# Shifted norms whose low parts come from the high parts, and a first slot pair that runs chunk by chunk

## The chip, the core and the metric

The kernel is one program on one NeuronCore of a Trainium2 chip. The metric is the device time of an execution in microseconds (us). The engines are named as in the profile: PE is TensorE (PEld its weight load), DVE is VectorE, ACT is ScalarE, POOL is GpSimd, SP is SyncE, which issues most of the transfers.

## What is computed

A chain of seven stages works on a matrix x of 256 tokens by 1024 features, in float32: a feed-forward block (`ffn1`), a mixer of attention over selected keys and a gated recurrence (`mix1`), a second feed-forward block (`ffn2`), and twice a three-part mixer (`mix2_l`) followed by a mixture over learned experts (`peer_l`). Every stage begins with a norm. In the first three it is modulated with a scale and a shift that come from a conditioning vector:

```python
def rmsnorm(x, g):
    y = xf * lax.rsqrt(jnp.mean(xf * xf, axis=-1, keepdims=True) + EPS)
    return (y * g.astype(jnp.float32)).astype(x.dtype)

def modulate(h, shift, scale):
    return h * (1 + scale[:, None, :]) + shift[:, None, :]

h = modulate(rmsnorm(x, mix_pre_g[l]), m[3], m[4])
proj = h @ w_in[l]
...
h = modulate(rmsnorm(x, ffn2_pre_g[l]), m[6], m[7])
y = swiglu(h, ffn2_w_gate[l], ffn2_w_up[l], ffn2_w_down[l])
...
u = rms_norm(x, attn_norm_w) @ w_in        # the later four stages: no shift
```

## The kernel before, in words

**Split products.** Each float32 product of matrices is made of three matmuls on rounded operands. A value v is kept as a high part, v rounded to the matmul's format, and a low part, v minus the high part. For weights W and activations H the kernel adds up hi(W)·hi(H), lo(W)·hi(H) and hi(W)·lo(H). The tiles of the weights are `whi` and `wlo`. Those of the normed activations are `HH` and `HL`, two views of one tile that the profile calls `HT`.

**Slots.** The weights of all stages come as one stream of 765 slots of 128x1024, two to a transfer of 1 MB into a `raw` buffer. For slot i, ACT copies `raw` to `whi` (`hi`, line 312), DVE (in some slots POOL) makes `wlo` (`lo`, line 331), and PE uses both. There are three buffers of each (`NSPLIT`), so that hi(i+3) waits until PE has used slot i. A slot's product with H has 8 chunks of 128 features, three matmuls each, in `chan`, lines 349 to 351. Each engine carries out its own instructions in the order in which the code issues them; what it needs of another engine it waits for on a semaphore.

**The start of a stage.** PE turns the normed rows into features by rows in PSUM (`norm_turn`, line 523), in 4 banks with 2 chunks each. Then `HH` and `HL` are made, one instruction for each chunk of 128x256:
- With a shift (`mix1` and `ffn2`; `ffn1` has its own opening): ACT makes all eight `HH` (line 547). DVE first makes lo of the second slot, then computes each chunk once more in full precision into `f` = x·gain + shift (line 574). The low part is f minus HH, a step of its own: for chunks 1, 3 and 7 on DVE (line 581), for chunks 0, 2, 4, 5 and 6 on POOL (line 589).
- Without a shift (the later four stages): ACT makes four `HH` (line 544), DVE the other four (line 560), and DVE makes each `HL` in one step as x·gain minus HH (line 570).

**The first two slots.** Of the six stages after `ffn1`, each gives its first two slots, i and i+1, to `chan_pair` (line 395): 48 matmuls for two outputs. They run in three passes over the eight chunks: hi(W)·HH, then lo(W)·HH, then hi(W)·HL. Slot i+2 is next on PE, with `chan`, and its first product waits for hi and lo of that slot. Behind the norm, DVE's next work is lo(i+2) in `ffn2` and in the later stages. In `mix1` there are two small instructions ahead of it, which split a weight `wi` that SP loads (lines 1551 and 1554; the transfer is issued at line 1285).

Of the kernel before, what the change touches and what calls it, by code (L numbers as in the profile page):

```python
# [4 lines left out]
F32 = mybir.dt.float32  # L5
# [5 lines left out]
ALU = mybir.AluOpType  # L11
# [143 lines left out]
class Program:  # L155
# [227 lines left out]
    def chan_pair(self, e, i, n, outs, banks):  # L383

        k, one = self.k, banks[0] == banks[1]
        for a, b in ((0, 0), (1, 0), (0, 1)):
            for c in range(8):
                s, h = slice(c * 128, c * 128 + 128), (self.HH, self.HL)[b]
                for j in range(2):
                    first, stop = (a, b, c) == (0, 0, 0), (a, b, c) == (0, 1, 7)  # L390
                    for w in k.late((("hi", "lo")[a], i + j), (("hh", "hl")[b], n, c),
                                    *(self.free[banks[j]] if first else [])):
                        e.wait_ge(*w)
                    part = (self.whi, self.wlo)[a][:, (i + j) % NSPLIT, :]
                    t = e.matmul(outs[j], part[:, s], h[:, c, :], start=first and not (j and one),  # L395
                                 stop=stop and (j == 1 or not one))
        t.then_inc(*k.inc("pe_used", ("used", i)))
        k.same(("used", i + 1), ("used", i))
# [151 lines left out]
    def norm_apply_dve(self, e, n, gain, shift, f, need, end):  # L550


        k = self.k
        if shift is None:
            self.lo(e, end + 1)
            for c in (2, 3, 6, 7):
                b = c // 2
                for w in k.late(self.turned(n, b), *need):
                    e.wait_ge(*w)
                e.tensor_scalar(self.HH[:, c, :], self.ps[:, b, 256 * (c % 2):256 * (c % 2) + 256], gain[:, c:c + 1], None,  # L560
                                ALU.mult).then_inc(*k.inc("dve_hh", ("hh", n, c)))
        else:
            self.lo(e, end + 1)
        for b in range(4):
            for c in (2 * b, 2 * b + 1):
                src, g = self.ps[:, b, 256 * (c % 2):256 * (c % 2) + 256], gain[:, c:c + 1]
                for w in k.late(self.turned(n, b), ("hh", n, 2 * b + 1), ("hh", n, c), *need):
                    e.wait_ge(*w)
                if shift is None:
                    e.scalar_tensor_tensor(self.HL[:, c, :], src, g, self.HH[:, c, :].bitcast(F32), ALU.mult,  # L570
                                           ALU.subtract).then_inc(*k.inc("dve_h", ("hl", n, c)))
                    k.same(("applied", n, b), ("hl", n, c))
                else:
                    e.tensor_scalar(f[:, c, :], src, g, shift[:, c:c + 1], ALU.mult,
                                    ALU.add).then_inc(*k.inc("dve_f", ("f", n, c)))
                    k.same(("applied", n, b), ("f", n, c))
            for c in (2 * b, 2 * b + 1):
                if shift is not None and c in (1, 3, 7):
                    for w in k.late(("f", n, c), ("hh", n, c)):
                        e.wait_ge(*w)  # L580
                    e.tensor_tensor(self.HL[:, c, :], f[:, c, :], self.HH[:, c, :].bitcast(F32),
                                    ALU.subtract).then_inc(*k.inc("dve_h", ("hl", n, c)))

    def norm_apply_pool(self, e, n, f):
        k = self.k
        for c in (0, 2, 4, 5, 6):
            for w in k.late(("f", n, c), ("hh", n, c)):
                e.wait_ge(*w)
            e.tensor_tensor(self.HL[:, c, :], f[:, c, :], self.HH[:, c, :].bitcast(F32),
                            ALU.subtract).then_inc(*k.inc("pool_h", ("hl", n, c)))  # L590

# [510 lines left out]
    def ffn_pool(self, e, t):  # L1104
        k, n, opens = self.k, NORM[t.tag], t.first > 0
        if opens:
            self.opening_pool(e, t)
        else:
            self.norm_apply_pool(e, n, t.f)
        if opens:  # L1110
            for b in range(2):
                self.bias_rows_pool(e, b)
            self.settle(e)
            e.tensor_scalar(self.norms[:, :, :], self.norms[:, :, :], D ** 0.5, None, ALU.mult).then_inc(*k.inc("pool_setup", "norms"))
            lc = self.lc
            e.tensor_scalar(lc[:, 0:4], self.vec("lam"), -1.0, None, ALU.mult).then_inc(*k.inc("pool_setup", "-lam"))
            for seg in range(5):
                self.softplus_pool(e, "lam", lc[:, 0:4], lc[:, 4:8], self.lc_sp, ["-lam"], seg)
            for w in k.late(("lam", "softplus")):
                e.wait_ge(*w)  # L1120
            e.tensor_scalar(lc[:, 0:4], lc[:, 4:8], -8.0, None, ALU.mult).then_inc(*k.inc("pool_setup", "lc a"))
            for w in k.late("lc a"):
                e.wait_ge(*w)
            e.tensor_scalar(lc[:, 4:8], lc[:, 0:4], 2.0, None, ALU.mult).then_inc(*k.inc("pool_setup", "lc"))
        for tt in range(2):
            self.sums_pool(e, ("res", n + 1, tt), self.st[:, tt, 1, :])
            self.sums_pool(e, (n + 1, tt), self.st[:, tt, 0, :])
        self.lo(e, t.down + F_CH + 1, True)
# [567 lines left out]
    def mixer1_pool(self, e):  # L1696
        k, t = self.k, self.m1
        n, tag = t.n, t.tag
        for w in k.late(("bias rows", 0), ("bias rows", 1)):
            e.wait_ge(*w)  # L1700
        self.norm_apply_pool(e, n, t.f)
        for w in k.late(("hh", n, 7), ("hl", n, 7)):
            e.wait_ge(*w)
        e.memset(t.SC[:, :, :], 0.0).then_inc(*k.inc("pool_index", (tag, "zero")))
# [1483 lines left out]
```

## Time and profile before

| | us |
|---|---|
| median of 3 runs (range) | 2466.11 (2465.45 to 2466.92) |
| the profiled execution's own time | 2468.6 |
| its span, first to last instruction | 2466.4 |
| PE matmuls busy | 2418.4 |
| DVE busy | 1801.5 |
| ACT busy | 1268.8 |
| POOL busy | 264.8 |

Matmuls are pipelined: a row's duration runs from its start to its modelled end, so that rows of PE overlap. A new matmul starts every 0.12 us or so where the moving operand has 256 columns. In rows of the timeline, "x16" is a run of 16 like instructions, and a bracket says how long the engine was idle ahead of the row and what ended that.

### The profile page before, as it was taken

To read this page: it belongs to the slowest core of one execution; us is meant where nothing else is said; L and a number is where in the kernel's file an instruction comes from. 1 tells how busy PE (TensorE), PEld (TensorE's weight loads), DVE (VectorE), ACT (ScalarE), POOL (GpSimd) and SP (SyncE) were. 2 spreads that over 40 slices of the span, in tenths; PEclk is the share of its full clock that TensorE was granted. 3 is DMA by queue.
4 is the path that set the end of the run, shared out by engine and by line. 5 is a ranking of instruction groups with operands and counts; after the bars stand their busy time and mean duration, and the time that the engine had idled before them with its cause. 6 is when DMAs were issued, how large, how long until landed. Compare 5 with 4: busy or idle time off the path is not lost.

```text
span 2466.4 us, 39282 instructions
## 1 busy us (share of the span) xinstructions
PE 2418.4 (98%) x15784; PEld 2102.4 (85%) x15784; DVE 1801.5 (73%) x3475; ACT 1268.8 (51%) x1811; POOL 264.8 (11%) x247
## 2 busy tenths in 40 slices
PE   7999999999999999999999999999999999999999
PEld 7987878988988888888888888988888888888887
DVE  8887666656756788888887556845778888888555
ACT  3544655445655565555444545654565555444444
POOL 3012101000203600000000000211720000000000
PEclk9999999999999999999999999999999999999999
DMA  9797334655324454444545555324454444445554
GB/s 388 264 341 256 122 123 174 222 197 176 127 107 173 175 192 181 171 171 156 186 171 201 196 190 197 138 103 170 173 188 172 174 170 171 171 174 185 205 190 151
DMA packets 73029, 455.77 MB, mean 185 GB/s; under 512 B 9099, under 2 KB 15371, under 8 KB 20754
## 3 DMA queue, kind: packets, MB, share of 16 engines
q1 hardware_dynamic: 72162, 452.21, 50.7%
q8 instruction: 127, 2.08, 0.3%
q0 software_dynamic: 688, 1.06, 0.3%
q14 instruction: 52, 0.43, 0.1%
HBM read 449.17 MB, written 4.06 MB: 184 GB/s over the span
## 4 chain that ended last, share of the span: by engine, by line
PE 89%; DVE 6%; ACT 3%; DMA 1%; issue 1%; POOL 1%; SPq 0%; DVEq 0%; ACTq 0%; POOLq 0%
PE ps L376 19%; PE ps L349 17%; PE ps L351 17%; PE ps L350 17%; PE ps L378 8%; PE ps L2559 2%; DVE wlo L331 2%; PE ps L375 1%; ACT whi L312 1%; DVE raw L342 1%; PE ps L395 1%; PE ps L1901 1%; DMA raw<-in_ffn_d 1%; PE ps L1151 1%; PE ps L2539 1%
## 5 line engine op out<-in xcount | busy, mean ns | idle before, releaser
L312 ACT ACTIVATE whi<-raw 128x1024 fp32r<-128x1024 f32 x765 | 809.5, 1060 | 1049.0 <-PE ps L351 639.5
L331 DVE TENSOR_TENSOR wlo<-raw,whi 128x1024 fp32r<-128x1024 f32 x700 | 856.6, 1227 | 516.0 <-ACT whi L312 515.6
L376 PE MATMUL ps<-HT,whi 128*128 128x512 f32 x2048 | 718.6, 399 | 0.0
L378 PE MATMUL ps<-HT,wlo 128*128 128x256 f32 x1792 | 502.1, 280 | 0.0
L376 PEld LDWEIGHTS ps<-HT,whi 128*128 128x128 f32 x2048 | 372.3, 188 | 68.9
L349 PE MATMUL ps<-whi,CT 128*128 128x512 f32 x1024 | 404.0, 395 | 1.2 <-DVE wlo L331 0.9
L350 PE MATMUL ps<-wlo,CT 128*128 128x512 f32 x1024 | 398.7, 389 | 0.0
L351 PE MATMUL ps<-whi,CT 128*128 128x512 f32 x1024 | 398.6, 389 | 0.0
L378 PEld LDWEIGHTS ps<-HT,wlo 128*128 128x128 f32 x1792 | 338.5, 189 | 8.6
L349 PE MATMUL ps<-HT,whi 128*128 128x256 f32 x968 | 277.9, 287 | 2.2 <-DVE wlo L331 1.2
L350 PE MATMUL ps<-HT,whi 128*128 128x256 f32 x968 | 274.5, 284 | 0.0
L351 PE MATMUL ps<-HT,wlo 128*128 128x256 f32 x968 | 274.3, 283 | 0.0
L351 PEld LDWEIGHTS ps<-whi,CT 128*128 128x128 f32 x1024 | 192.2, 188 | 40.3
L349 PEld LDWEIGHTS ps<-whi,CT 128*128 128x128 f32 x1024 | 192.3, 188 | 40.0 <-issue 2.6
L350 PEld LDWEIGHTS ps<-wlo,CT 128*128 128x128 f32 x1024 | 192.5, 188 | 37.8
L349 PEld LDWEIGHTS ps<-HT,whi 128*128 128x128 f32 x968 | 184.7, 191 | 7.5 <-issue 4.6
L350 PEld LDWEIGHTS ps<-HT,whi 128*128 128x128 f32 x968 | 184.7, 191 | 0.5
L351 PEld LDWEIGHTS ps<-HT,wlo 128*128 128x128 f32 x968 | 184.7, 191 | 0.5
L331 POOL TENSOR_TENSOR wlo<-raw,whi 128x1024 fp32r<-128x1024 f32 x65 | 157.4, 2424 | 163.4 <-ACT whi L312 163.4
L2870 DVE TENSOR_TENSOR AST<-AST,ps 128x512 f32<-128x512 f32 x128 | 87.4, 683 | 60.3 <-ACT AST L2669 60.3
L480 POOL TENSOR_SCALAR st<-st 128x1 f32<-128x1 f32 x20 | 8.6, 432 | 917.8 <-ACT xn L472 710.2
L2853 DVE TENSOR_TENSOR OJ<-EQ,GP 128x512 f16<-128x512 f16 x256 | 97.4, 422 | 4.4
(397 smaller groups left out, 3282.1 us busy)
## 6 DMA issues: line engine op xcount, KB each, us to landing
raw<-in_down SPq DMA_DIRECT2D x128, 1024.0 KB, 4.8
raw<-in_up SPq DMA_DIRECT2D x128, 1024.0 KB, 4.8
raw<-in_w_in SPq DMA_DIRECT2D x41, 1024.0 KB, 4.8
raw<-in_ffn_gu SPq DMA_DIRECT2D x36, 1024.0 KB, 4.9
raw<-in_w_ada SPq DMA_DIRECT2D x28, 1024.0 KB, 7.0
raw<-in_ffn_d SPq DMA_DIRECT2D x22, 1024.0 KB, 5.8
raw<-in_w_out SPq DMA_DIRECT2D x12, 1024.0 KB, 4.8
raw<-in_w_ada SPq DMA_DIRECT2D x16, 512.0 KB, 12.6
```

The lines of the kernel that those rows point to most:

```text
L312: e.activation(self.whi[:, i % NSPLIT, :], self.raw_of(i), ACT.Copy, bias=0.0, scale=1.0).then_inc(*k.inc("w_hi", ("hi", i)))
L331: e.tensor_tensor(self.wlo[:, n, :], self.raw_of(i), self.whi[:, n, :].bitcast(F32), ALU.subtract).then_inc(*k.inc("w_lo_pool" if pool els ...
L342: e.tensor_tensor_reduce(out=raw[:, a, :], in0=raw[:, a, :], in1=self.cb[:, :], scale=1.0, scalar=0.0, op0=ALU.mult, op1=ALU.add, accum_ou ...
L349: e.matmul(out, lh, rh, start=first, stop=False)
L350: e.matmul(out, lh, rl, start=False, stop=False)
L351: return e.matmul(out, ll, rh, start=False, stop=stop)
L375: e.matmul(out[:, 0:T], lo[:, s], self.HH[:, c, :], start=False, stop=False)
L376: t = e.matmul(out.rearrange("p (a t) -> p a t", a=2), hi[:, s], self.HT[:, c, :, :], start=c == 0, stop=c == 7)
L378: t = e.matmul(out[:, 0:T], lo[:, s], self.HH[:, c, :], start=False, stop=False)
L2559: m = e.matmul(PS[:, b, 64 * x:64 * x + 64], t.OI[s % 2][:, x // 2, :, x % 2], t.OJ[s % 2][:, p, x // 2, :, x % 2], start=p == 0, stop=p == 1)
L2853: e.tensor_tensor(t.OJ[c][:, p, :, :, :], t.EQ[:, :, :, :], spread(t.GP[:, p, :], 64), ALU.mult).then_inc(*k.inc("dve_gates", (tag, "one j ...
L2870: e.tensor_tensor(a, a, PS[:, b:b + 2, 0:T], ALU.add).then_inc(*k.inc("dve_sums", (tag, "sum", p)))
```

## The change

There are two edits. In the shifted norms, POOL now computes f = HH - shift for all eight chunks, with one tensor input and one scalar for each partition, and DVE makes every low part in one step as x·gain - f, which is what the norms without a shift do with HH in place of f. `HL` no longer comes from POOL. A PSUM bank of the norm is now free after DVE's last `HL` of it, where it was free after the last `f`. In `chan_pair`, hi(W)·HH and lo(W)·HH now go together chunk by chunk, and the pass over hi(W)·HL stays at the end.

```diff
@@ chan_pair
-        for a, b in ((0, 0), (1, 0), (0, 1)):
-            for c in range(8):
+        for a, b, cs in [(a, 0, (c,)) for c in range(8) for a in range(2)] + [(0, 1, range(8))]:
+            for c in cs:
@@ norm_apply_dve
+        self.lo(e, end + 1)
         if shift is None:
-            self.lo(e, end + 1)
...
-        else:
-            self.lo(e, end + 1)
         for b in range(4):
             for c in (2 * b, 2 * b + 1):
...
-                if shift is None:
-                    e.scalar_tensor_tensor(self.HL[:, c, :], src, g, self.HH[:, c, :].bitcast(F32), ALU.mult,
-                                           ALU.subtract).then_inc(*k.inc("dve_h", ("hl", n, c)))
-                    k.same(("applied", n, b), ("hl", n, c))
-                else:
-                    e.tensor_scalar(f[:, c, :], src, g, shift[:, c:c + 1], ALU.mult,
-                                    ALU.add).then_inc(*k.inc("dve_f", ("f", n, c)))
-                    k.same(("applied", n, b), ("f", n, c))
-            for c in (2 * b, 2 * b + 1):
-                if shift is not None and c in (1, 3, 7):
-                    for w in k.late(("f", n, c), ("hh", n, c)):
-                        e.wait_ge(*w)
-                    e.tensor_tensor(self.HL[:, c, :], f[:, c, :], self.HH[:, c, :].bitcast(F32),
-                                    ALU.subtract).then_inc(*k.inc("dve_h", ("hl", n, c)))
+                x, ready = (self.HH[:, c, :].bitcast(F32), ("hh", n, c)) if shift is None else (f[:, c, :], ("f", n, c))
+                for w in k.late(ready):
+                    e.wait_ge(*w)
+                e.scalar_tensor_tensor(self.HL[:, c, :], src, g, x, ALU.mult,
+                                       ALU.subtract).then_inc(*k.inc("dve_h", ("hl", n, c)))
+                k.same(("applied", n, b), ("hl", n, c))
@@ norm_apply_pool
-        for c in (0, 2, 4, 5, 6):
-            for w in k.late(("f", n, c), ("hh", n, c)):
-                e.wait_ge(*w)
-            e.tensor_tensor(self.HL[:, c, :], f[:, c, :], self.HH[:, c, :].bitcast(F32),
-                            ALU.subtract).then_inc(*k.inc("pool_h", ("hl", n, c)))
+        for c in range(8):
+            for w in k.late(("hh", n, c)):
+                e.wait_ge(*w)
+            e.tensor_scalar(f[:, c, :], self.HH[:, c, :].bitcast(F32), shift[:, c:c + 1], None,
+                            ALU.subtract).then_inc(*k.inc("pool_f", ("f", n, c)))
```

This is DVE's order in the norm of `mix1` before. HT_69 is the tile of HH and HL, f_119 is f, md_83 holds gain and shift, and wlo_68 is the slots' low part:

```order
L331 TENSOR_TENSOR wlo_68<-raw_54,whi_67 128x1024 [waits w_hi,bias1,bias0]
L574 TENSOR_SCALAR f_119<-ps,md_83 128x256 [waits dve_gate,act_h,pe_norm]
L574 TENSOR_SCALAR f_119<-ps,md_83 128x256
L581 TENSOR_TENSOR HT_69<-f_119,HT_69 128x256 [waits dve_f]
L574 TENSOR_SCALAR f_119<-ps,md_83 128x256 [waits act_h,pe_norm]
...
L581 TENSOR_TENSOR HT_69<-f_119,HT_69 128x256 [waits dve_f]
L1551 CAST wih_135<-wi_134 128x64 [waits ld_m1w]
L1554 TENSOR_TENSOR wil_136<-wi_134,wih_135 128x64 [waits dve_index]
L331 TENSOR_TENSOR wlo_68<-raw_55,whi_67 128x1024 [waits w_hi] x2
```

The same place after the change:

```order
L331 TENSOR_TENSOR wlo_68<-raw_54,whi_67 128x1024 [waits w_hi,bias1,bias0]
L570 SCALAR_TENSOR_TENSOR HT_69<-ps,md_83,f_119 128x256 [waits dve_gate,pool_f,act_h,pe_norm]
L570 SCALAR_TENSOR_TENSOR HT_69<-ps,md_83,f_119 128x256 [waits pool_f]
L570 SCALAR_TENSOR_TENSOR HT_69<-ps,md_83,f_119 128x256 [waits pool_f,act_h,pe_norm]
...
L570 SCALAR_TENSOR_TENSOR HT_69<-ps,md_83,f_119 128x256 [waits pool_f]
L1542 CAST wih_135<-wi_134 128x64 [waits ld_m1w]
L1545 TENSOR_TENSOR wil_136<-wi_134,wih_135 128x64 [waits dve_index]
L331 TENSOR_TENSOR wlo_68<-raw_55,whi_67 128x1024 [waits w_hi] x2
```

Eleven instructions of DVE have become eight, each of which waits for POOL, and lo(i+2) still stands behind the last of them (in `mix1` behind the two on `wi` as well).

On PE, the pair's first matmuls in `mix1` before, where `act_h` is the wait for the next HH and `w_lo_dve` that for lo of the two slots:

```order
L395 MATMUL ps<-HT_69,whi_67 128x256 [waits dve_res,w_hi]
L395 MATMUL ps<-HT_69,whi_67 128x256 [waits act_h]
L395 MATMUL ps<-HT_69,whi_67 128x256
...
L395 MATMUL ps<-HT_69,wlo_68 128x256 [waits w_lo_dve] x2
L395 MATMUL ps<-HT_69,wlo_68 128x256 x14
L395 MATMUL ps<-HT_69,whi_67 128x256 [waits pool_h]
```

And after:

```order
L395 MATMUL ps<-HT_69,whi_67 128x256 [waits dve_res,w_hi]
L395 MATMUL ps<-HT_69,wlo_68 128x256 [waits w_lo_dve] x2
L395 MATMUL ps<-HT_69,whi_67 128x256 [waits act_h]
L395 MATMUL ps<-HT_69,whi_67 128x256
L395 MATMUL ps<-HT_69,wlo_68 128x256 x2
...
L395 MATMUL ps<-HT_69,whi_67 128x256 [waits dve_h]
```

The sixteen matmuls of the second pass have moved up between those of the first, two behind each pair, and the wait for lo of slot i+1 has moved from the 17th matmul to the third.

## Rows read from the trace of the kernel before

**Rows 1.** The page: busy us of PE, its share, instructions.

```profile
PE 2418.4 (98%) x15784; PEld 2102.4 (85%) x15784; DVE 1801.5 (73%) x3475; ACT 1268.8 (51%) x1811; POOL 264.8 (11%) x247
```

**Rows 2.** Waits of PE: for whom, us in total, times, longest.

```profile
PE ps L349 <- DVE wlo L331: 2.1, 4, 0.9
```

**Rows 3.** Timeline, PE's weight loads, `mix1`: the pair, then slot i+2.

```profile
228.42 0.74 PEld L395 LDWEIGHTS ps<-HT,whi 128*128 128x128 f32 x4 [0.67 <-issue]
...
231.83 1.97 PEld L395 LDWEIGHTS ps<-HT,wlo 128*128 128x128 f32 x16
233.73 1.99 PEld L395 LDWEIGHTS ps<-HT,whi 128*128 128x128 f32 x16
236.83 0.19 PEld L349 LDWEIGHTS ps<-HT,whi 128*128 128x128 f32 x1 [1.11 <-issue]
```

**Rows 4.** Timeline of `mix1`: ACT, POOL, SP and DVE around the norm.

```profile
227.79 3.76 ACT L547 ACTIVATE HT<-ps,md 128x256 fp32r<-128x256 f32 x8 [0.71 <-PE ps L523]
...
232.46 2.34 POOL L589 TENSOR_TENSOR HT<-f,HT 128x256 fp32r<-128x256 f32 x3 [0.82 <-DVE f L574]
...
229.00 0.43 SPq L1285 DMA_DIRECT2D wi<-in_w_idx  x1
...
234.98 0.34 DVE L1551 CAST wih<-wi 128x64 fp32r<-128x64 f32 x1 [0.78 <-DMA wi<-in_w_idx]
...
235.50 1.22 DVE L331 TENSOR_TENSOR wlo<-raw,whi 128x1024 fp32r<-128x1024 f32 x1
```

**Rows 5.** Timeline, PE's weight loads, `ffn2`: the pair, then slot i+2.

```profile
388.73 0.74 PEld L395 LDWEIGHTS ps<-HT,whi 128*128 128x128 f32 x4 [0.26 <-issue]
...
396.46 0.19 PEld L349 LDWEIGHTS ps<-HT,whi 128*128 128x128 f32 x1 [0.45 <-issue]
```

**Rows 6.** Timeline of `ffn2`: ACT, DVE and POOL around the norm.

```profile
388.09 3.76 ACT L547 ACTIVATE HT<-ps,md 128x256 fp32r<-128x256 f32 x8 [0.30 <-PE ps L523]
391.70 1.09 ACT L312 ACTIVATE whi<-raw 128x1024 fp32r<-128x1024 f32 x1
...
394.25 0.42 DVE L581 TENSOR_TENSOR HT<-f,HT 128x256 fp32r<-128x256 f32 x1
394.59 1.76 DVE L331 TENSOR_TENSOR wlo<-raw,whi 128x1024 fp32r<-128x1024 f32 x1
...
392.93 2.34 POOL L589 TENSOR_TENSOR HT<-f,HT 128x256 fp32r<-128x256 f32 x3 [0.82 <-DVE f L574]
```

**Rows 7.** Timeline, `mix2_0` and `peer_0`: DVE's lo(i+2), PE's first load of slot i+2.

```profile
591.86 1.21 DVE L331 TENSOR_TENSOR wlo<-raw,whi 128x1024 fp32r<-128x1024 f32 x1
593.18 0.19 PEld L349 LDWEIGHTS ps<-HT,whi 128*128 128x128 f32 x1
...
749.13 1.22 DVE L331 TENSOR_TENSOR wlo<-raw,whi 128x1024 fp32r<-128x1024 f32 x1
750.47 0.19 PEld L349 LDWEIGHTS ps<-HT,whi 128*128 128x128 f32 x1
```

**Rows 8.** Instructions by line: ns of one, min/median/max; first and last start.

```profile
L547 ACT ACTIVATE HT<-ps,md x16: 557/574/600, 227.8 to 391.3; 128x256 fp32r<-128x256 f32 x16
L589 POOL TENSOR_TENSOR HT<-f,HT x10: 730/742/944, 230.0 to 394.3; 128x256 fp32r<-128x256 f32 x10
L480 POOL TENSOR_SCALAR st<-st x20: 297/382/1046, 8.6 to 1682.4; 128x1 f32<-128x1 f32 x20
L490 POOL TENSOR_SCALAR ms<-ms x4: 193/193/194, 694.1 to 1635.9; 128x2 f32<-128x2 f32 x4
L570 DVE SCALAR_TENSOR_TENSOR HT<-ps,norms,HT x32: 470/474/478, 588.6 to 1689.4; 128x256 fp32r<-128x256 f32 x32
```

**Rows 9.** Groups by line: POOL's memsets, busy us, mean ns.

```profile
L2425 POOL MEMSET AT<- 128x1024 f32 x2 | 1.9, 955 | 0.0
L1704 POOL MEMSET SC<- 128x512 f32 x1 | 0.5, 517 | 0.0
```

**Rows 10.** Window, `ffn2` from slot i+2: its length; PE, PEld, DVE, ACT, POOL busy (count).

```profile
396.46:579.60 183.14, 183.10 (x1287) 172.24 (x1288) 105.95 (x138) 83.80 (x117) 0.86 (x2) 1.00 0.57 207
```

More of the change, by code:

```diff
@@ L568, in norm_apply_dve, with norm_apply_pool @@
                     e.wait_ge(*w)
-                if shift is None:
-                    e.scalar_tensor_tensor(self.HL[:, c, :], src, g, self.HH[:, c, :].bitcast(F32), ALU.mult,
-                                           ALU.subtract).then_inc(*k.inc("dve_h", ("hl", n, c)))
-                    k.same(("applied", n, b), ("hl", n, c))
-                else:
-                    e.tensor_scalar(f[:, c, :], src, g, shift[:, c:c + 1], ALU.mult,
-                                    ALU.add).then_inc(*k.inc("dve_f", ("f", n, c)))
-                    k.same(("applied", n, b), ("f", n, c))
-            for c in (2 * b, 2 * b + 1):
-                if shift is not None and c in (1, 3, 7):
-                    for w in k.late(("f", n, c), ("hh", n, c)):
-                        e.wait_ge(*w)
-                    e.tensor_tensor(self.HL[:, c, :], f[:, c, :], self.HH[:, c, :].bitcast(F32),
-                                    ALU.subtract).then_inc(*k.inc("dve_h", ("hl", n, c)))
-    def norm_apply_pool(self, e, n, f):
+                x, ready = (self.HH[:, c, :].bitcast(F32), ("hh", n, c)) if shift is None else (f[:, c, :], ("f", n, c))
[4 more added lines that the diff above has]
+                k.same(("applied", n, b), ("hl", n, c))
+    def norm_apply_pool(self, e, n, f, shift):
         k = self.k
-        for c in (0, 2, 4, 5, 6):
-            for w in k.late(("f", n, c), ("hh", n, c)):
+        for c in range(8):
+            for w in k.late(("hh", n, c)):
                 e.wait_ge(*w)
-            e.tensor_tensor(self.HL[:, c, :], f[:, c, :], self.HH[:, c, :].bitcast(F32),
-                            ALU.subtract).then_inc(*k.inc("pool_h", ("hl", n, c)))
+            e.tensor_scalar(f[:, c, :], self.HH[:, c, :].bitcast(F32), shift[:, c:c + 1], None,
+                            ALU.subtract).then_inc(*k.inc("pool_f", ("f", n, c)))
     def gate_dve(self, e, tag, m, scale, post, v, dg):
@@ L1108, in ffn_pool @@
         else:
-            self.norm_apply_pool(e, n, t.f)
+            self.norm_apply_pool(e, n, t.f, self.md[:, 8:16])
         if opens:
@@ L1700, in mixer1_pool @@
             e.wait_ge(*w)
-        self.norm_apply_pool(e, n, t.f)
+        self.norm_apply_pool(e, n, t.f, self.md[:, 8:16])
         for w in k.late(("hh", n, 7), ("hl", n, 7)):
```

## The prediction

> **What bounds the kernel now.** I read the page first. PE's matmuls are busy for 2418.4 of the 2466.4 us of the span, 98% [rows 1], so no other engine's busy time matters by itself; only what makes PE stand still can be won back, and the 48 us outside of that share are all there is. I then read the list of what PE waits for. One line in it belongs to the places that the change touches: `chan`'s first matmul waits for a slot's low part four times, 2.1 us in all [rows 2]. So I went through the timeline at all six stage starts that use `chan_pair`, to see what releases slot i+2.
>
> In `mix1` the pair's first weight load is at 228.42, its second pass at 231.83, its third at 233.73, and slot i+2 begins at 236.83 [rows 3]. The second pass takes 1.90 us for 16 matmuls, 0.119 each. The first pass has as many and takes 3.41, because ACT gives it one HH in 0.455 us (eight take 3.76, one takes 0.574 [rows 4, 8]) and it needs one in 0.24. Here 1.5 us are idle in pieces, and the new order fills exactly these: four matmuls to a chunk are 0.475 us of work, a little more than ACT's pace.
>
> But PE does not go on when the pair is done. In `mix1` the last pass would end at 233.73 + 1.90 = 235.63, and slot i+2 begins 1.2 us later. What it waits for is DVE's lo(i+2), 235.50 + 1.22 = 236.72 [rows 4], and the load comes 0.11 behind that. It is the same at the others. In `ffn2` lo(i+2) ends at 394.59 + 1.76 = 396.35 and the load is at 396.46 [rows 5, 6]. In `mix2_0` it ends at 593.07 and the load is at 593.18, in `peer_0` at 750.35 and 750.47 [rows 7]; `mix2_1` and `peer_1` repeat these two. Six times of six, PE's next slot starts 0.10 to 0.12 us behind the end of lo(i+2). **The end of the stage's start is therefore set by DVE's queue, and not by the pair.**
>
> **The change, part by part.**
>
> *The pair in a new order, six times.* It ends the pair up to 1.5 us sooner in `mix1` and `ffn2`, and about 0.2 in the four others. I cost it at nothing by itself, since lo(i+2) does not move with it. What hides it is that wait; if the cover were gone, it would be worth those amounts. Its own risk is that lo of slot i+1 is now needed by the third matmul, 0.24 us behind the first, and not by the 17th. It is in DVE's queue ahead of the norm, and the trace has it done before the first or at its start, so I take no loss.
>
> *The norms without a shift, four times.* Their instructions stay as they are, and DVE's queue too: nothing.
>
> *The norm of `ffn2`.* Call p the time of POOL's new step. The first HH ends at 388.09 + 0.57 = 388.66 [rows 6, 8]. A hand-over costs the 0.11 seen above. POOL then runs eight steps in a row, since ACT's pace of 0.455 is shorter than any p I consider, and the last f ends at 388.77 + 8p. DVE's last HL ends 0.11 + 0.47 behind it, by the same instruction in the norms without a shift [rows 8], at 389.35 + 8p. Lo(i+2) starts 0.08 before its forerunner's end, as it does now (394.25 + 0.42 against 394.59 [rows 6]), takes 1.22, and PE loads 0.11 later, at **390.60 + 8p**, against 396.46 now. ACT's hi(i+2) is ready at 392.79 [rows 6] and doesn't count. PE itself can't be there before 388.73 + 3 x 1.90 = 394.43, so at most 2.0 us are to be had.
>
> *How long is p?* No row shows a POOL instruction with one tensor input of this size. From below: POOL's memsets take 517 ns for 512 columns and 955 for 1024 [rows 9], 0.855 ns a column, and a step that also reads should not be faster. Its short steps with one input take 0.193 us where the scalars are constants, and from 0.297 where one scalar comes from a tile, as here [rows 8]. That gives 0.193 + 0.22 = 0.41 or 0.297 + 0.22 = 0.515. From above: the step that it replaces, with two tensor inputs and the same shape, has a median of 0.742 [rows 8]. The new one reads one stream, where the memset reads none and the old step reads two. The row with the tile's scalar is the nearest in kind, so I go a third of the way from 0.515 to 0.742 and take p = 0.59. PE then loads at 395.32, 1.14 us sooner. At 0.515 it is 1.74, at 0.41 the 2.0 of PE's own limit, at 0.742 it is 0.08 too late.
>
> The Trainium skill ("GPSIMD Engine Reference", section on elementwise cycle accounting) puts GpSimd at about 2.6 cycles an element with two tensor inputs and at 1.8 at best in an ordinary loop, and its table of engine selection gives elementwise work to VectorE. The old step's 0.742 for 256 columns agrees with its two-input figure. By its 1.8, an estimate from the page, p would be about 0.38 + 0.30 = 0.68 and `ffn2` would win 0.4.
>
> *Lo(i+2) itself.* It took 1.76 us in `ffn2` and 1.22 in `mix1`. In `ffn2` it started while POOL was still in its low parts (392.93 + 2.34 = 395.27), in `mix1` after them (POOL's row ends at 234.80) [rows 4, 6]. In the changed kernel POOL is done 0.5 us before it starts, so I use 1.22; if it stayed at 1.76, 0.54 of the gain would go. The Trainium skill ("SBUF — State Buffer", "Who interferes with whom") says that a DVE instruction with two inputs in SBUF contends with a GpSimd instruction that reads SBUF; these two rows agree.
>
> *The norm of `mix1`.* By the same steps the last HL ends at 229.05 + 8p, 233.77 for p = 0.59. Behind it in DVE's queue stands the cast of `wi`, which waits for a transfer: SP issued it at 229.00 and it landed at 234.98 [rows 4]. SP was held there by a transfer of the weights' stream, and not by anything of the norm. So the cast stays at 234.98, lo(i+2) at 235.50, and PE at 236.83: nothing, as long as 228.97 + 8p stays under 234.98, that is p under 0.75. DVE only waits longer for the same transfer.
>
> *Is the lead kept?* From slot i+2 of `ffn2` to the end of its products the window is 183.14 us long and PE is busy in 183.10 [rows 10]. PE alone sets the pace there, so a start that is sooner by 1.14 should come out whole.
>
> **Sum.** `ffn2` -1.14, all else 0. On the profiled execution that is 2468.6 - 1.1 = 2467.5; its own time lies 2.5 above the median of the runs, so on the median it is 2466.1 - 1.1 = **2465.0 us**. A difference under 0.2%, 4.9 us, can hardly be told from none here.
>
> **The rivals.**
> - *POOL's step is near the old one's, p from 0.67 to 0.78.* The gain is gone: from 0.5 us to a loss of 0.7, around 2466.0. For it: POOL's shortest steps already vary, from 0.297 to 1.046 [rows 8]. Against it: one stream less to read. Chance 0.17.
> - *The other side: POOL becomes the bound.* Eight steps in a row replace five that were shared with DVE. In `ffn2` the loss begins at p = 0.73, in `mix1` at 0.75, and from there each 0.1 costs 0.8 us in each. At 0.944, the slowest old step [rows 8], that is 1.7 and 1.5, 3.2 us together: 2469.3. Slower by over 0.2% needs p over 1.04. For it: no row excludes a slow form of this instruction. Against it: DVE's new steps read PSUM and one tile, where the old ones read two. Chance 0.08.
> - *`mix1` gains too.* If `wi` landed sooner than the norm's end, the cast would start at 233.69 and PE would win another 1.3 us: 2463.7. Against it: the transfer is issued at a time that the change doesn't touch. Chance 0.05.
> - *The lead is lost.* The 1.14 us run into a later wait that doesn't move with PE, or the pair's new order costs a small wait for lo(i+1) at six places. 2466.1. Against it stands the gapless window. Chance 0.15.
>
> **How the numbers follow.** The forecast (p from 0.47 to 0.67, 2464.1 to 2465.6) has 0.55. The rest is above. To the cases I add the 0.75 us by which medians of these runs scatter: the range is 2463.0 to 2467.5, which leaves out the slow POOL and part of the tails. All cases but the far end of the slow POOL lie within 4.9 us: same 0.95, faster 0.02, slower 0.03.
>
> **What the new profile would show.** POOL's eight steps on `f` at 0.5 to 0.67 us each; the pair's loads without gaps, its third pass 1.3 us or more sooner in both stages; in `ffn2` lo(i+2) at 1.22 us from about 394.0 and slot i+2 near 395.3; in `mix1` DVE idle for over a microsecond ahead of the cast, and slot i+2 where it was. In all six stages slot i+2 should follow the end of lo(i+2) by 0.11. The prediction is wrong if POOL's step is over 0.75, if slot i+2 of `mix1` moves, or if a stage without a shift moves.

## The result, and the profile after

The changed kernel takes 2469.5 us (2467.34 to 2475.01, 15 executions), where the kernel before takes 2465.61 (2464.47 to 2467.84, 15 executions beside it). The ratio is 1.0019, with a 95% interval of 1.0012 to 1.0026. The forecast was 2465.0 with a range up to 2467.5, and "slower by over 0.2%" had 3 in 100; the time lies 2.0 us above the range and 3.9 above the kernel before. At 0.19% it is just short of that 0.2%.

The profiled execution of the changed kernel is the longest of the fifteen, 2475.01 us, with a span of 2473.1. Its mean granted clock is 0.994, where the profile of before has 0.997, so its stage starts are read here apart from its total.

The page after, against [rows 1] (busy us of each engine, share of the span, instructions):

```profile
PE 2424.2 (98%) x15784; PEld 2109.0 (85%) x15784; DVE 1797.7 (73%) x3469; ACT 1268.6 (51%) x1811; POOL 274.0 (11%) x253
```

PE has as many matmuls as before and is busy 5.8 us longer. So a part of the loss is matmuls that run slower, and not a wait. POOL has six instructions more and 9.2 us more.

The list of what PE waits for, after, against [rows 2] (us in total, times, the longest):

```profile
PE ps L349 <- DVE wlo L331: 3.4, 5, 1.6
PE ps L395 <- DVE HT L570: 2.9, 8, 0.5
```

The wait for slot i+2's low part has grown from 2.1 to 3.4 us. The pair itself now waits eight times for DVE's `HL`, 2.9 us.

The timeline of `mix1` after, against [rows 3, 4]:

```profile
226.40 3.75 ACT L547 ACTIVATE HT<-ps,md 128x256 fp32r<-128x256 f32 x8 [0.71 <-PE ps L523]
227.03 0.31 PEld L395 LDWEIGHTS ps<-HT,whi 128*128 128x128 f32 x2 [0.67 <-issue]
227.52 7.25 POOL L580 TENSOR_SCALAR f<-HT,md 128x256 f32<-128x256 f32 x8 [2.58 <-ACT HT L547]
230.62 0.31 PEld L395 LDWEIGHTS ps<-HT,wlo 128*128 128x128 f32 x2
230.86 1.19 PEld L395 LDWEIGHTS ps<-HT,whi 128*128 128x128 f32 x8
232.74 0.30 PEld L395 LDWEIGHTS ps<-HT,whi 128*128 128x128 f32 x2 [0.70 <-DVE HT L570]
...
234.81 0.48 DVE L570 SCALAR_TENSOR_TENSOR HT<-ps,md,f 128x256 fp32r<-128x256 f32 x1 [0.32 <-POOL f L580]
235.34 0.30 PEld L395 LDWEIGHTS ps<-HT,whi 128*128 128x128 f32 x2 [0.50 <-DVE HT L570]
235.37 0.56 DVE L1542 CAST wih<-wi 128x64 fp32r<-128x64 f32 x1
236.10 1.22 DVE L331 TENSOR_TENSOR wlo<-raw,whi 128x1024 fp32r<-128x1024 f32 x1
237.44 0.29 PEld L349 LDWEIGHTS ps<-HT,whi 128*128 128x128 f32 x1 [1.79 <-issue]
```

POOL's eight steps take 7.25 us, 0.906 each. (This is the row's length over eight. A single step lasts 0.914 to 0.944, since they overlap a little.) The 32 products with `HH` run from 227.03 to 230.86 without a gap, as the new order should have it, but the third pass then goes at POOL's pace: its last four chunks come 0.8 to 1.0 us apart, where PE needs 0.24. DVE's row at 234.81 was idle for 0.32 ahead of it until POOL's `f` came. The cast now stands straight behind the last `HL`: `wi` was issued at 227.60 and landed 7.7 us later, at about the time at which that `HL` ends. And slot i+2 is again 0.12 behind the end of lo(i+2), 237.32. From the pair's first load to that of slot i+2 it is now 10.41 us, against 8.41 before.

The timeline of `ffn2` after, against [rows 5, 6]:

```profile
392.45 0.30 PEld L395 LDWEIGHTS ps<-HT,whi 128*128 128x128 f32 x2 [0.25 <-issue]
392.48 7.26 POOL L580 TENSOR_SCALAR f<-HT,md 128x256 f32<-128x256 f32 x8 [1.72 <-ACT HT L547]
...
399.77 0.48 DVE L570 SCALAR_TENSOR_TENSOR HT<-ps,md,f 128x256 fp32r<-128x256 f32 x1 [0.32 <-POOL f L580]
400.17 1.22 DVE L331 TENSOR_TENSOR wlo<-raw,whi 128x1024 fp32r<-128x1024 f32 x1
401.50 0.29 PEld L349 LDWEIGHTS ps<-HT,whi 128*128 128x128 f32 x1 [0.90 <-issue]
```

The same picture without the cast: eight steps in 7.26 us, lo(i+2) at 1.22 us and no longer 1.76, slot i+2 0.11 behind it, and 9.05 us from pair to slot against 7.73 before. The two places together have lost 2.00 + 1.32 = 3.3 us.

The rest is in the windows around them (length; PE busy and matmuls; granted clock, DMA share, GB/s):

```profile
222.00:232.00 10.00, 8.47 (x68) 1.00 0.41 152
232.00:237.44 5.44, 2.27 (x10) 0.94 1.15 210
237.44:243.40 5.96, 5.93 (x28) 0.50 1.01 254
...
392.40:401.50 9.10, 7.16 (x49) 0.95 0.44 155
401.50:407.40 5.90, 5.87 (x27) 0.50 0.46 160
```

The same stretches of the kernel before, from its slot i+2 on, and one near its start:

```profile
236.83:242.80 5.97, 5.94 (x49) 1.00 1.14 214
396.46:402.40 5.94, 5.91 (x49) 1.00 0.40 141
20.00:30.00 10.00, 6.50 (x34) 0.68 1.03 410
```

Behind the slow third pass, in which PE was busy for 2.27 of 5.44 us, the granted clock is 0.50 for about 6 us, the lower of its two levels (1.2 GHz and not 2.4). PE gets through 28 matmuls at 0.213 us each and not through 49 at 0.122. At the higher level 28 would take 3.4, so 2.6 us are lost, and as much again in `ffn2`. The lower level itself is not new: the profile of the kernel before has it too, from 23.5 to 30.4 us and from 306.8 to 313.7, away from both places. New in this profile is that it stands behind both pairs.

Only the mean clock is on record for the other executions. Nine of the fifteen have a mean clock of 0.996 to 0.998 and a median of 2469.12 us, which is 3.5 above the kernel before: about the 3.3 us of the two places. The other six have 0.994 or 0.995 and a median of 2473.5, another 4.4 above; the profiled one is among them. That the lower clock stands at the same places in the other five is likely, but not shown. In the 87 executions of the kernel before that were timed beside the kernels below, none was below 0.996.

### The profile page after: what moved, and what is told of

It reads as the page before. It is cut to its first block, busy times and chain, and to the rows that moved or that the text cites. A ratio compares the mean times of both kernels' runs of the same rounds, so it can differ in the third digit from the quotient of the medians.

```text
span 2473.1 us, 39271 instructions
## 1 busy us (share of the span) xinstructions
PE 2424.2 (98%) x15784; PEld 2109.0 (85%) x15784; DVE 1797.7 (73%) x3469; ACT 1268.6 (51%) x1811; POOL 274.0 (11%) x253
## 4 chain that ended last, share of the span: by engine, by line
PE 88%; DVE 6%; ACT 3%; DMA 1%; POOL 1%; issue 1%; SPq 0%; DVEq 0%; ACTq 0%; POOLq 0%
PE ps L376 19%; PE ps L349 17%; PE ps L350 17%; PE ps L351 17%; PE ps L378 8%; PE ps L2550 2%; DVE wlo L331 2%; PE ps L375 1%; ACT whi L312 1%; DVE raw L342 1%; PE ps L1892 1%; PE ps L395 1%; PE ps L1142 1%; DMA raw<-in_ffn_d 1%; PE ps L2530 1%
```

## The experiments

The theory after the result: POOL's step is the whole cause of the longer distances. It takes 0.906 us for a chunk and not 0.59, so that it, and not ACT or DVE, sets when `HL` and with it lo(i+2) are done; the pair's new order costs nothing by itself. The rivals: that the new order of the pair loses the time, or that POOL's step is slow only because DVE works beside it. The distances are from the pair's first load to that of slot i+2 in the profile of each kernel, us; the last column is what both have lost or won together. The time's difference is that of the median to the kernel before on the same chip.

| kernel | `mix1` | `ffn2` | median (range) | ratio [95%] | to before | both places |
|---|---|---|---|---|---|---|
| before | 8.41 | 7.73 | | | | |
| after | 10.41 | 9.05 | 2469.5 | 1.0019 [1.0012, 1.0026] | +3.9 | +3.3 |
| e1 pair's order alone | 8.51 | 7.74 | 2466.36 (2464.21 to 2470.94) | 1.0000 [0.9991, 1.0009] | 0.0 | +0.1 |
| e2 norms alone | 9.90 | 9.07 | 2469.65 (2467.46 to 2471.51) | 1.0011 [1.0002, 1.0020] | +3.3 | +2.8 |
| e3 constant in place of the shift | 9.75 | 8.40 | 2467.97 (2465.55 to 2470.74) | 1.0006 [0.9997, 1.0015] | +1.6 | +2.0 |
| e4 PE filled | 11.09 | 11.08 | 2471.39 (2470.02 to 2473.58) | 1.0021 [1.0012, 1.0030] | +5.0 | +6.0 |
| e5 PE lightly filled | 9.88 | 9.06 | 2468.37 (2466.28 to 2470.24) | 1.0008 [0.9999, 1.0017] | +1.9 | +2.8 |
| e7 broadcast operand | 9.17 | 6.39 | 2465.3 (2463.06 to 2468.63) | 0.9998 [0.9989, 1.0007] | -0.6 | -0.6 |
| v1 pair's order, late cast | 7.56 | 7.73 | 2464.8 (2462.58 to 2466.88) | 0.9991 [0.9982, 1.0000] | -1.6 | -0.9 |
| v2 v1, more on GpSimd | 8.59 | 7.69 | 2465.79 (2464.59 to 2467.32) | 0.9998 [0.9989, 1.0007] | -0.7 | +0.1 |
| v3 e7 and late cast | 6.84 | 6.39 | 2462.59 (2460.49 to 2463.54) | 0.9984 [0.9975, 0.9993] | -3.3 | -2.9 |
| v4 v3, old order of the pair | 7.21 | 7.22 | 2464.65 (2462.79 to 2467.26) | 0.9993 [0.9984, 1.0002] | -1.3 | -1.7 |

Each median but that of "after" is over 11 executions, for which the interval of the ratio reaches about 2.2 us to each side. Only those of the changed kernel, e2, e4 and v3 leave out 1. The last two columns agree within 1.1 us in every row, so within that scatter the two distances account for the times.

**e1, the pair's order alone.** The kernel before, with this:

```diff
@@ chan_pair
-        for a, b in ((0, 0), (1, 0), (0, 1)):
-            for c in range(8):
+        for a, b, cs in [(a, 0, (c,)) for c in range(8) for a in range(2)] + [(0, 1, range(8))]:
+            for c in cs:
```

Expected:

> The kernel before with the new order of the pair alone. Theory A (GpSimd's step of 0.906 us lengthens VectorE's queue, and the pair's order moves nothing): slot i+2 still starts 0.11 us behind the end of lo(i+2) in all six stages, at the old distance from the pair's start or up to 0.1 less; time 2465.6, within 1 us of before, clock as before. Theory B (the new order is what costs, because PE ends two passes early and then stands): the pair to slot i+2 takes 1 us or more longer in mix1 and ffn2, granted clock falls behind it, time 2468 to 2470.

The list of what PE waits for, in this kernel, and two windows of `mix1`, whose slot i+2 loads at 234.40:

```profile
PE ps L349 <- DVE wlo L331: 3.0, 5, 1.4
...
230.00:235.00 5.00, 3.04 (x19) 0.96 1.11 248
235.00:240.00 5.00, 5.00 (x33) 0.70 1.15 220
```

Slot i+2 stayed where it was at both places (+0.10 and +0.01 us), and the wait for lo(i+2) grew from 2.1 us to 3.0: what the pair wins is waited for there. The ratio is 1.0000. The order is not the cause of the longer distances, and with it alone the time is the same within 2.2 us, as the prediction's zero says.

The clock was not as expected, though. It is 0.50 from 234.6 to 238.0 in this profile, right behind the pair of `mix1`, with POOL's old steps. Ahead of that PE had stood still three times, the last time for 1.36 us. The profile of before has 1.00 there. So the lower clock behind a pair does not need POOL's slow step. Over the whole execution the mean clock is 0.997, as before, since this profile lacks the stretch near the start.

**e2, the norms alone.** The changed kernel with `chan_pair` as before (the diff of e1 the other way round).

Expected:

> The changed norms with the old order of the pair. Theory A: GpSimd takes 7.2 us for its eight steps as in the changed kernel, and slot i+2 is late by 2.0 us in mix1 and 1.2 in ffn2; with the clock's share about that of the changed kernel, 2468.5 to 2470. If the stop-and-go of the third pass is what lowers the clock, the old order has less of it (the first two passes take 1.4 us longer), so the clock falls later or less, and the time is 2468.5 to 2469. Theory B: 2466 or less.

The timeline of `mix1` in this kernel, and a window from 1.2 us ahead of its slot i+2 at 236.22:

```profile
226.82 7.28 POOL L580 TENSOR_SCALAR f<-HT,md 128x256 f32<-128x256 f32 x8 [2.59 <-ACT HT L547]
...
235.00:240.00 5.00, 3.92 (x33) 1.00 1.15 196
```

2.8 us at the two places and 3.3 in the median: the norms alone make all of the loss of the changed kernel's nine executions at 0.996 and more. None of the eleven here was below 0.997, and behind both pairs the clock is 1.00 in this profile. Executions at 0.994 or 0.995 are on record only for kernels that have the new order and the new norms together (the changed kernel, e3, e7).

**e3, a constant in place of the shift.** The changed kernel, whose POOL step takes a number from the instruction and not from a tile. It leaves the shift out.

```diff
-            e.tensor_scalar(f[:, c, :], self.HH[:, c, :].bitcast(F32), shift[:, c:c + 1], None,
+            e.tensor_scalar(f[:, c, :], self.HH[:, c, :].bitcast(F32), 0.25, None,
```

Expected:

> The changed kernel with GpSimd subtracting the constant 0.25 where it subtracted the shift from a tile, so the shift is wrong in the two norms' low parts; all else stays. If the scalar from a tile makes GpSimd's step slow, it falls from 0.906 to 0.4 to 0.6 us, slot i+2 of ffn2 comes 1 us or more sooner than before and the time is 2464 to 2465. If the step is slow for its size and input alone, it stays at 0.85 to 0.91 and the time at 2469 to 2470.

The timeline of `mix1` in this kernel:

```profile
226.21 6.60 POOL L580 TENSOR_SCALAR f<-HT 128x256 f32<-128x256 f32 x8 [2.59 <-ACT HT L547]
```

A step takes 0.825 us, between the two values expected and 0.08 less than in the changed kernel, and slot i+2 of `ffn2` comes 0.65 sooner than in the changed kernel, which is eight times that. Two of its eleven executions have a clock of 0.995. So the distance follows p with the slope of 8 that the prediction gave it. But the tile's scalar is only a small part of the price: 0.825 is itself above the 0.73 from which the loss begins.

**e4 and e5, PE filled in the third pass.** They ask whether the granted clock falls because PE stands still there. Both are the changed kernel with matmuls of the identity into a PSUM bank that nobody reads:

```diff
@@ chan_pair, in the loop over c; e5 (e4: c > 1, and 4 products)
+                if n in (1, 2) and b == 1 and c > 3:
+                    self.bank(e, 7)
+                    for _ in range(2):
+                        e.matmul(self.ps[:, 7, 128:256], self.ident[:, :], self.ident[:, :], start=True, stop=True)
```

Expected of e4:

> The changed kernel with four small matmuls into an unused bank ahead of each of the last six chunks of the third pass in the two shifted norms, so that PE doesn't stand between them. If part of the loss is PE's clock, halved for 6 us behind each of the two gappy passes, the clock behind them stays at 1.0, 2 to 2.6 us come back for each place in executions that had it, and the time falls to 2467.5 to 2469, with the late lo(i+2) left. If the clock has another cause, it falls all the same, and the time is 2469.5 or more.

Each of these products is two matmuls in the trace, 0.112 us from start to start, so that a chunk got 0.90 us of filling and not the half of it. With its own two products a chunk took PE 1.13 us, more than POOL's 0.906: PE was its own bound in the third pass, and lost 3.35 us in `ffn2`. The time, expected at 2467.5 to 2469, came out at 2471.39 for that reason and says nothing of the clock, which was 1.00 behind both pairs. So e5 has two products, ahead of the last four chunks alone. What was expected of it reckons with 0.119 us for a short matmul, where the trace has 0.112:

> The changed kernel with two filler products (four short matmuls, 0.48 us) ahead of each of the last four chunks of the third pass in the two shifted norms; the heavier filling before showed eight of 0.119 us per chunk and held PE up itself. Theory A with the clock as the second part of the loss: slot i+2 stays where lo(i+2) puts it (9.9 to 10.4 us behind the pair's start in mix1, 9.1 in ffn2), the clock behind the pairs stays at 1.0, no execution is at a granted clock of 0.994, and the median is 2468.5 to 2469.2. If the clock falls for another reason, executions at 0.994 near 2473 are there as in the changed kernel.

The windows around the two places in e5, columns as above:

```profile
227.00:237.05 10.05, 8.69 (x64) 1.00 0.97 254
237.05:243.05 6.00, 5.97 (x50) 1.00 1.08 253
...
397.88:403.88 6.00, 5.97 (x50) 1.00 0.48 169
```

The distances are those of e2 (9.88 and 9.06), so the filling cost nothing. The clock stayed at 1.00 behind both pairs, and none of the eleven executions was below 0.997, where six of fifteen of the changed kernel were. The median lies 1.9 us above before, against 3.9. That speaks for it that PE's standing still brings the lower clock. It isn't settled: the intervals of the two ratios overlap, and e2, in which PE has no filling but waits for `HL` only 1.1 us in all and not 2.9, since its first passes end later, had no such execution either. Over all profiles, the clock is 0.50 for 3.4 us around the start of slot i+2 in `mix1` in e1, e3, e7 and v2 too, all with the new order. It doesn't in e4 and e5, which have the filling, in v1 and v3, which have the new order as well, nor in before, e2, e6 and v4, with the old order. In `ffn2` it is low there in the changed kernel alone. This is one execution of each, so it shows that the fall is not bound to POOL's slow step, and not what decides on it.

**e6, POOL's instructions one by one.** The kernel before, with groups of eight steps (four at 512 columns) on `f` behind the norm of `ffn2`, each group waiting for the one before. It was timed once, at 2466.92 us.

```diff
+        for c in range(8):
+            t = e.tensor_scalar(f[:, c, :], f[:, c, :], shift[:, c:c + 1], None, ALU.subtract)
+        ...
+        for c in range(8):
+            t = e.tensor_tensor(f[:, c, :], f[:, c, :], shift[:, c:c + 1].to_broadcast([P, T]), ALU.subtract)
```

Expected:

> The kernel before with groups of eight GpSimd instructions on f right behind the norm of ffn2, each kind on a line of its own; nothing waits for them. It prices the step by itself, with VectorE making nothing of the norm. If the step of 0.906 us is GpSimd's own price, the tensor_scalar with a tile's scalar has 0.85 to 0.91 here too, the one with a constant 0.75 to 0.83, and 128x512 twice the slope of 128x256. If VectorE's reads of f slowed it in the changed kernel, its shortest here is 0.5 to 0.7.

The instructions by line in this kernel (ns of one, min/median/max; first and last start; shape). DVE and POOL's own further work go on beside them and stretch some, so the shortest is the one to read:

```profile
L603 POOL TENSOR_SCALAR f<-f,md x8: 920/1186/2657, 393.7 to 404.2; 128x256 f32<-128x256 f32 x8
L606 POOL TENSOR_SCALAR f<-f x8: 843/1107/1553, 405.2 to 412.6; 128x256 f32<-128x256 f32 x8
L609 POOL TENSOR_TENSOR f<-f x8: 607/903/1592, 414.1 to 421.8; 128x256 f32<-128x256 f32 x8
L612 POOL TENSOR_SCALAR f<-f,md x4: 1562/2026/2412, 422.5 to 428.1; 128x512 f32<-128x512 f32 x4
L618 POOL COPY f<-f x8: 393/1210/1397, 439.8 to 447.0; 128x256 f32<-128x256 f32 x8
L621 POOL TENSOR_SCALAR f<-f,md x8: 598/606/1360, 447.5 to 453.1; 128x128 f32<-128x128 f32 x8
L624 POOL TENSOR_TENSOR f<-f,md x8: 608/700/1691, 453.8 to 460.1; 128x256 f32<-128x256 f32 x8
```

By the shortest of each, TENSOR_SCALAR with the tile's scalar takes 0.598 us for 128 columns, 0.920 for 256 and 1.562 for 512: 2.5 ns a column and 0.28 fixed. With a constant it is 0.843, the copy is 0.393, and TENSOR_TENSOR, which reads two operands, is 0.607. It stays at 0.608 where its second operand is the shift's one column, repeated 256 times by the address. The two values for TENSOR_SCALAR lie 0.01 above what was expected. The rival of DVE's work beside it falls: the shortest of eight is as long as the steps of the changed kernel. There the first step of `mix1` took 0.944 us, the longest of the sixteen, while DVE was idle (its first `HL` starts at 228.59). It is the form of the instruction that is slow.

**e7, the same subtraction in the other form.** The changed kernel, with

```diff
-            e.tensor_scalar(f[:, c, :], self.HH[:, c, :].bitcast(F32), shift[:, c:c + 1], None,
+            e.tensor_tensor(f[:, c, :], self.HH[:, c, :].bitcast(F32), shift[:, c:c + 1].to_broadcast([P, T]),
                             ALU.subtract)
```

Expected:

> The changed kernel with GpSimd's step written as a tensor_tensor whose second operand is the shift's column repeated 256 times: the same values, another form. In the probe that form took 0.608 us at its shortest and tensor_scalar 0.920. If p, GpSimd's time for a step, is what decides, the eight steps take 4.9 to 5.5 us in place of 7.25, and by the prediction's own sum (1.87 + 8p from the pair's start) slot i+2 of ffn2 starts 6.75 to 7.2 us behind the pair's start, before 7.73, changed kernel 9.05. In mix1 wi's transfer holds it at 8.4. Time 0.5 to 1 us under before, and no execution at a granted clock of 0.994. If something else in the new norm costs the time, it stays at 2468 or more.

The timeline of this kernel, `mix1` and then `ffn2`:

```profile
232.89 0.20 DVE L1542 CAST wih<-wi 128x64 fp32r<-128x64 f32 x1 [1.88 <-DMA wi<-in_w_idx]
...
387.68 4.62 POOL L580 TENSOR_TENSOR f<-HT,md 128x256 f32<-128x256 f32 x8 [1.70 <-ACT HT L547]
394.06 0.19 PEld L349 LDWEIGHTS ps<-HT,whi 128*128 128x128 f32 x1 [0.59 <-issue]
```

A step is 0.577 us, almost the 0.59 of the prediction, and `ffn2` wins 1.34 where the prediction had 1.14 for 0.59. Its distance of 6.39 lies below the 6.75 expected, because that took 0.61 and more for a step. In `mix1` DVE stands idle for 1.88 us ahead of the cast, until `wi` lands: the prediction's picture of that place. The distance there is 0.76 longer than before, since the transfer was issued at 226.13 and landed 6.7 us later, where it took 6.0 before [rows 4]; 8.4 was expected. Together that is -0.6 us, and the median says -0.6, which by itself is not clear of none. One of the eleven executions has a clock of 0.995.

**v1, a late cast.** e1, and in `mix1` lo(i+2) ahead of the two steps on `wi`:

```diff
         self.norm_apply_dve(e, n, self.md[:, 0:8], self.md[:, 8:16], t.f, [("gain", 3)], t.slot)
+        self.lo(e, t.slot + 2)
         for w in k.late("w_idx in"):
```

Expected:

> The kernel before with the new order of the pair, and in mix1 VectorE makes lo(i+2) ahead of the two small steps on wi, so that it no longer waits for wi's transfer. If VectorE's queue sets the start of slot i+2 in mix1, lo(i+2) starts right behind the last low part, 1.3 us sooner, takes up to 1.76 us beside GpSimd, and the pair to slot i+2 falls from 8.4 to 7.2 to 7.7 us; ffn2 stays at 7.7. Time 0.7 to 1.2 us under before. If the pair's order or the transfer mattered otherwise, there is no gain.

The timeline of `mix1` in this kernel:

```profile
232.40 1.75 DVE L331 TENSOR_TENSOR wlo<-raw,whi 128x1024 fp32r<-128x1024 f32 x1
234.08 0.18 DVE L1552 CAST wih<-wi 128x64 fp32r<-128x64 f32 x1
```

`mix1` wins 0.85 us, as expected; the median wins 1.6, with an interval that reaches 1.0000. It would be 0.5 more if lo(i+2) had stayed at 1.22. It now starts beside POOL's last low parts, which end at 233.07, and takes 1.75, as it did in `ffn2` before [rows 6]. The rule of the Trainium skill ("SBUF — State Buffer", "Who interferes with whom") by which the two contend agrees with these rows again.

**v2, more of the old subtractions on GpSimd.** v1, with POOL making `HL` of chunks 0 to 6 from `f` and DVE only that of chunk 7:

```diff
-                if shift is not None and c in (1, 3, 7):
+                if shift is not None and c == 7:
...
-        for c in (0, 2, 4, 5, 6):
+        for c in range(7):
```

Expected:

> As the version before it, and GpSimd subtracts the low parts of chunks 0 to 6 in the old two-step form, VectorE only that of chunk 7. GpSimd has idle gaps of 0.8 us between its steps now, so the two more fit in. VectorE's queue is then shorter by 0.9 to 1.1 us. Expected: the pair to slot i+2 at 7.0 us in ffn2 (from 7.7) and 7.0 to 7.6 in mix1, bounded by GpSimd's last step; time 1.3 to 2 us under before. If GpSimd's seventh step becomes the bound (over 0.78 us each), ffn2 stays at 7.5 or more and the gain is that of the version before alone.

The timeline of `mix1` in this kernel:

```profile
226.40 6.11 POOL L589 TENSOR_TENSOR HT<-f,HT 128x256 fp32r<-128x256 f32 x7 [3.71 <-DVE f L574]
231.82 0.30 PEld L395 LDWEIGHTS ps<-HT,whi 128*128 128x128 f32 x2 [1.37 <-POOL HT L589]
```

Of the two cases expected the second came, and `mix1` is worse than either. Seven steps take 6.11 us, 0.87 each in the mean: their median is still 0.742, but the longest, beside lo(i+2), takes 1.70. POOL is the bound, and PE waits for it 1.37 us at one load. `mix1` is 1.03 longer than in v1, which is more than v1 had won there.

**v3, both, and v4, v3 without the new order.** v3 is e7 with the late cast of v1. v4 is v3 with `chan_pair` as before.

Expected of v3:

> The run before it with lo(i+2) ahead of the two steps on wi in mix1. VectorE's queue is then the same in both stages: slot i+2 at 6.75 to 7.2 us behind the pair's start in both. Time 2 to 2.7 us under before. If the transfer of wi didn't hold mix1, there is no difference to the run before it.

Expected of v4:

> The run before it with the old order of the pair. Now VectorE's queue is short enough for PE's own passes to count: 3.41 + 1.90 + 1.99 = 7.3 us from the pair's start, before slot i+2. If so, slot i+2 comes at 7.3 in both stages, 0.1 to 0.55 us later each than with the new order, 0.2 to 1.1 us in all. If the pair's order is worth nothing even here, the times agree.

The timeline of v3, `mix1` and then `ffn2`:

```profile
226.91 4.62 POOL L580 TENSOR_TENSOR f<-HT,md 128x256 f32<-128x256 f32 x8 [2.56 <-ACT HT L547]
231.96 1.22 DVE L331 TENSOR_TENSOR wlo<-raw,whi 128x1024 fp32r<-128x1024 f32 x1
233.29 0.19 PEld L349 LDWEIGHTS ps<-HT,whi 128*128 128x128 f32 x1 [0.90 <-issue]
233.94 0.20 DVE L1543 CAST wih<-wi 128x64 fp32r<-128x64 f32 x1 [0.76 <-DMA wi<-in_w_idx]
...
391.91 0.19 PEld L349 LDWEIGHTS ps<-HT,whi 128*128 128x128 f32 x1 [0.59 <-issue]
```

POOL is done at 231.53, before lo(i+2) starts, so that lo(i+2) is again at 1.22, and the wait for `wi` now stands behind it, where PE doesn't wait for it. v3 takes 2462.59 us, 0.9984 [0.9975, 0.9993] of the kernel before, and its interval lies wholly below that of the changed kernel. It beats both. Against the kernel before it wins 3.3 us in the median, where 2 to 2.7 were expected. v4 shows that the pair's new order is then worth 0.37 + 0.83 = 1.2 us at the two places (2.1 in the medians, with intervals that overlap), where in e1 it was worth nothing.

## Why the prediction was wrong

**The step that failed** is p, in "How long is p?". The prediction took 0.59 and called the old step's median of 0.742 a bound "from above", because the new step "reads one stream, where the memset reads none and the old step reads two". It measured 0.906 in both stages, and 0.920 at the shortest in e6. Two of the prediction's own signs of being wrong were there: the step was over 0.75, and slot i+2 of `mix1` moved. The cost of a POOL instruction doesn't go by the number of its tensor inputs: the one-input form with a scalar is slower than the two-input form of the same size. The bounds from below held, but the value was set too near to them: the short steps gave the fixed part (0.30; e6: 0.28), and the memsets did not give the slope (0.855 ns a column; e6: 2.5). The estimate from the Trainium skill ("GPSIMD Engine Reference", elementwise cycle accounting), 0.68, fell short as well, and the measurement decides.

**The sum around it held.** With 0.906 put in, "390.60 + 8p" gives 397.85 for `ffn2`, 1.39 later than before. Measured was 1.32. e3 and e7 confirm the slope: at 0.825 the formula gives 0.74 later, measured 0.67; at 0.577 it gives 1.24 sooner, measured 1.34.

**`mix1`** was to lose nothing up to p = 0.75 and 0.8 us for each 0.1 above, which is 1.24 at 0.906. e2 and e5 lose 1.5. Its sentence on `wi` took the landing as given; over the thirteen profiles the transfer took 5.9 to 7.7 us. One part that the prediction missed is the hand-over to POOL: its first step starts 1.12 us behind ACT's first in `mix1` (226.40 to 227.52), where it is 0.67 in `ffn2` and the prediction had 0.68 for both. Against that the cast is shorter when it has nothing to wait for. What holds POOL's first step in `mix1` for 0.45 us wasn't found; the trace names ACT's `HH`. In the profile of the changed kernel the loss is 2.0: there `wi` lands with the last `HL`, so that the cast starts 0.08 us behind the end of that `HL` (in e2 0.08 ahead of it), and beside POOL's memset it takes 0.56 and not 0.18.

**The pair at nothing** was right for the time of e1, and right for the reason given: slot i+2 stands 0.10 to 0.12 behind lo(i+2) in the changed kernel too, and e1 turns the pair's gain into a longer wait. The clause "if the cover were gone, it would be worth those amounts" was right in kind as well (v3 against v4).

**The norms without a shift** didn't move: in `peer_0` lo(i+2) ends at 757.75 and slot i+2 loads at 757.87.

**The rival that came true** is "The other side: POOL becomes the bound", with 0.08. It gave 3.2 us for p = 0.944. e2 shows it, with 2.8 us at the two places for 0.906 to 0.91. That the difference stays under 0.2%, as 0.95 said, is in part luck: it is 3.9 us of 4.9, of which the prediction's sum at p = 0.906 gives 2.6.

**Two small slips** bear on nothing. ACT's pace of 0.455 is not "shorter than any p I consider", since 0.41 is among them, and at p = 0.78 the sum loses 0.6 us and not 0.7.

**What no case held** is the clock. In the profiled execution the slow third pass is followed by about 6 us at half of it, at both places, and the six of fifteen executions with a mean clock like this one's take 4.4 us more. It moves the median by 0.4 (2469.5 against 2469.12) and the top of the range by five. The prediction asked only when slot i+2 would start, and not how PE would run behind a stretch in which it is busy for 2.3 of 5.4 us. That e5, which fills the stretch, shows none of it is evidence for this cause, not proof. And e1 has 3.4 us of it behind the pair of `mix1` with POOL's old steps, so the new order may have a part in it that its zero left out. What decides on the fall stays open.

## What to carry to other kernels

Before an instruction is moved to another engine, its price there has to be read from a row of the same form, with the same kind of scalar and the same size. Where no row has it, a form that reads more is not a bound from above, and the point at which the sum turns (here 0.73, against 0.59) should be held against the full spread of what is unknown. A gain that a queue covers, as that of the pair's order here, isn't lost: once the queue is short, it comes back, so that two edits are to be tried together before one is dropped. And a wait for a transfer belongs behind the work that the critical engine needs, not ahead of it.

## What the runs showed of the hardware

- GpSimd's TENSOR_SCALAR on 128x256 float32 takes 0.906 us a step in a row of eight, and 0.914 or more by itself, with a scalar for each partition, and 0.825 and 0.843 with a constant (after, e3, e6). From 128 to 512 columns it grows by 2.5 ns a column (e6). TENSOR_TENSOR takes 0.607 at its shortest where both operands are one tile (e6), 0.577 in a row of eight and 0.608 by itself where the second is one column repeated (e7, e6), and 0.742 with two tiles, written in the rounded format [rows 8]; the shortest copy took 0.393 (e6). The broadcast form does the same subtraction in less than two thirds of the time.
- The granted clock was 0.50 for some 6 us behind a pass in which PE was busy for 2.27 of 5.44 us, at two places of one execution of the changed kernel, and for 3.4 us at the end of the pair of `mix1` in e1, e3, e7 and v2. With short products put into such a pass it was 1.00 (e4, e5).
- A matmul of float32 with the 128x128 identity was two matmuls in the trace, 0.112 us from start to start (e4).
- DVE's lo took 1.75 us beside POOL's two-tile steps and 1.22 without (v1, v3), and a two-tile step beside it up to 1.70 (v2).
- A transfer of 32 KB, issued right behind others, landed 5.9 to 7.7 us later (v1, after).
